# Feed-forward gate and up: both products with the weights' rounded half as one product of 512 columns, its two halves added on ScalarE and VectorE

## The reference

```python
def _swiglu(h, w_gate, w_up, w_down):      # h [256, 1024], inner width 2816
    return (silu(h @ w_gate) * (h @ w_up)) @ w_down

for l in range(2):
    mod = silu(c) @ w_mod[l] + b_mod[l]     # 9 rows of 1024: shift, scale, gate, three times
    x = x + 0.5 * g1 * _swiglu(_rmsnorm_2(x) * (1 + sc1) + sh1, gate1, up1, down1)
    x = x + g2 * _hybrid_mixer(...)
    x = x + 0.5 * g3 * _swiglu(_rmsnorm_2(x) * (1 + sc3) + sh3, gate2, up2, down2)
```

## Time and profile before

| | us |
|---|---|
| median of 3 runs | 1724.25 (1721.18 to 1724.79) |
| the profiled execution: its own time | 1718.4 |
| its span, first to last instruction | 1716.4 |
| TensorE, VectorE, ScalarE, GpSimd busy in the span | 1568.0, 979.8, 602.5, 205.0 |
| granted TensorE clock, mean over the span | 0.953 |

### The profile page before, as it was taken

One profiled execution on the slowest core, in us unless ns is written; L12 is line 12 of the kernel. 1 busy time (PEld: TensorE's weight loads), 2 busy tenths in 40 slices (PEclk: granted clock), 3 DMA queues, 4 the chain that ended last, 5 costly groups with the idle time before them and its releaser, 6 DMA issues.

```text
span 1716.4 us, 21728 instructions
## 1 busy us (share of the span) xinstructions
PE 1568.0 (91%) x8944; PEld 1232.6 (72%) x8944; DVE 979.8 (57%) x1482; ACT 602.5 (35%) x944; POOL 205.0 (12%) x205
## 2 busy tenths in 40 slices
PE   7997779898779998999989998989989999989998
PEld 1646356546459996786459997789977865479986
DVE  0376776767247776355427777677774453354444
ACT  2335121142134442253224443344433541144442
POOL 0021142000001110033001110001100241001100
PEclk9998979996799999999999999999999999989999
DMA  9444324166247877332337787668874323355551
GB/s 344 145 128 142 98 74 148 62 220 216 78 150 254 285 269 279 104 132 74 123 98 245 258 310 272 240 197 270 284 297 168 109 88 99 109 161 184 185 172 49
DMA packets 192106, 305.44 MB, mean 178 GB/s; under 512 B 6140, under 2 KB 116488, under 8 KB 191880
## 3 DMA queue, kind: packets, MB, share of 16 engines
q1 hardware_dynamic: 189088, 299.45, 51.5%
q10 hardware_dynamic: 2919, 4.61, 0.7%
HBM read 302.99 MB, written 1.05 MB: 177 GB/s over the span
## 4 chain that ended last, share of the span: by engine, by line
PE 76%; DVE 11%; ACT 7%; issue 2%; DMA 2%; POOL 1%; ACTq 0%; DVEq 0%; POOLq 0%
PE ps L373 75%; DVE accs L514 2%; PE ps L376 1%; DVE wlo L1948 1%; ACT whi L1906 1%; DMA ring<-in_ffn_w_down_dram 1%; DMA ring<-in_w_mod_dram 1%; DVE arena L1205 1%; DVE arena L1202 1%; DVE H L1729 1%; ACT arena L1440 0%; DVE H L1795 0%; POOL misc L1776 0%; DVE misc L1507 0%; ACT hhi L1911 0%
## 5 line engine op out<-in xcount | busy, mean ns | idle before, releaser
L1948 DVE TENSOR_TENSOR wlo<-ring,whi 128x1024 fp32r<-128x1024 f32 x264 | 322.6, 1225 | 235.4 <-ACT whi L1906 230.4
L373 PE MATMUL ps<-hhi,whi 128*128 128x256 f32 x1408 | 405.4, 288 | 21.2 <-DVE hlo L1954 16.0
L373 PE MATMUL ps<-hlo,whi 128*128 128x256 f32 x1408 | 401.8, 285 | 0.0
L373 PE MATMUL ps<-hhi,wlo 128*128 128x256 f32 x1408 | 401.6, 285 | 0.0
L1906 ACT ACTIVATE whi<-ring 128x1024 fp32r<-128x1024 f32 x264 | 275.2, 1055 | 310.0 <-PE ps L373 280.2
L373 PEld LDWEIGHTS ps<-hhi,whi 128*128 128x128 f32 x1408 | 273.9, 195 | 23.1 <-DVE hlo L1954 21.9
L373 PEld LDWEIGHTS ps<-hlo,whi 128*128 128x128 f32 x1408 | 274.0, 195 | 1.2 <-issue 1.2
L373 PEld LDWEIGHTS ps<-hhi,wlo 128*128 128x128 f32 x1408 | 273.7, 194 | 0.0
L373 PE MATMUL ps<-ring,H 128*128 128x512 f32 (+1 forms) x608 | 262.9, 583 | 11.0 <-ACT arena L2083 5.6
L373 PEld LDWEIGHTS ps<-ring,H 128*128 128x128 f32 x608 | 113.1, 193 | 129.4 <-issue 114.1
L514 DVE SCALAR_TENSOR_TENSOR accs<-ring,misc,accs 128x512 f32<-128x512 f32 x266 | 201.3, 757 | 3.0
(11 more groups left out here) (288 smaller groups left out, 1398.9 us busy)
## 6 DMA issues: line engine op xcount, KB each, us to landing
ring<-in_w_mod_dram SPq DMA_DIRECT2D x84, 1024.0 KB, 7.3
ring<-in_w_in_dram SPq DMA_DIRECT2D x48, 1024.0 KB, 5.0
ring<-in_ffn_w_gate_dram SPq DMA_DIRECT2D x44, 1024.0 KB, 6.8
ring<-in_ffn_w_up_dram SPq DMA_DIRECT2D x44, 1024.0 KB, 5.4
ring<-in_ffn_w_down_dram SPq DMA_DIRECT2D x44, 1024.0 KB, 6.6
ring<-in_w_out_dram SPq DMA_DIRECT2D x12, 1024.0 KB, 4.9
gates<-in_b_mod_dram SPq DMA_DIRECT2D x7, 512.0 KB, 6.6
ring<-in_w_proj_a_dram SPq DMA_DIRECT2D x2, 1024.0 KB, 5.9
```

The source lines that it names most:

```text
L373: return self.e.matmul(o, lhsT, rhs, start=start, stop=stop)
L1948: v.done(v.e.tensor_tensor(lo, M.slot(key)[:, r0:r0 + rn, :], plain(hi), ALU.subtract), ("split", l, sub, n), *([M.freed(key)] if ends els ...
```

## The change

- The two products that use whi become one: hhi and hlo now lie in one tensor (`HH`, 2 x 8 x 256), and one product of 512 columns takes both. `wlo*hhi` stays a product of 256 columns. So per weight block there are two products in place of three.
- A tile now needs two banks, one for gate and one for up. In each, columns 0 to 255 hold `whi*hhi + wlo*hhi` and columns 256 to 511 `whi*hlo`. The pool "ga" has six banks, handed out by two: a pair takes four. They are asked for one tile at a time, at q = 0.
- The two halves have to be added: ScalarE copies columns 256 to 511 of both banks to a scratch tile of 2 x 256 (128 x 512 elements), VectorE adds columns 0 to 255 of both banks to it and frees the banks. Silu is then taken from the scratch tile, in place, and the mult reads both halves of the scratch tile.
- Order: on both engines the work on a pair's results now comes before the piece q = 3 of the next pair instead of behind it, and goes by kinds: ScalarE copy, copy, silu, silu, ahi, ahi; VectorE add, add, mult, mult. The first tile is announced by TensorE before the second has ended.

```diff
 POOLS:
-"ga": (0, 1, 2, 3),
+"ga": range(6),
 Store:
-        self.HHI, self.HLO = self.sbr("hhi", [128, 8, 256]), self.sbr("hlo", [128, 8, 256])
+        self.HH = self.sbr("hh", [128, 2, 8, 256])
+        self.HHI, self.HLO = self.HH[:, 0, :, :], self.HH[:, 1, :, :]
 def spare(M):
-    return [M.H[:, k, 256:512] for k in range(8)]
+    return [M.H[:, 2 * i:2 * i + 2, 256:512] for i in range(3)]
...
     ps_ = pieces(l, sub)
     for f in range(0, 22, 2):
         for q in range(4):
+            if q == 3:
+                yield f
             if f < 20:
                 emit(ps_[4 * (f // 2) + 4 + q])
             elif q < 3:
                 emit(ps_[44 + q])
             if work is not None:
                 tick(work, beside(f, q))
-        yield f
     emit(ps_[47])
     for kt in range(19):
         yield ("down", kt)
...
 def act_ffn(a, l, sub):
     M = a.M
-    SG = spare(M)[0:3]
+    SG = spare(M)
     def emit(p):
         n, key, r0, rn, wd_, _ = p
...
     for p in first[1:]:
         emit(p)
     for f in split_all(a, l, sub, emit, None):
-        for j in range(2 if isinstance(f, int) else 0):
-            i, key = (f + j) % 3, ("gu", l, sub, f + j)
-            a.wait_ge(("gu", l, sub, f), ("alo", l, sub, f + j - 3))
-            a.done(a.e.activation(SG[i], M.ps(key)[:, 0:256], ACT.Silu), ("silu", l, sub, f + j))
+        pair = range(f, f + 2) if isinstance(f, int) else ()
+        for x in pair:
+            key = ("gu", l, sub, x)
+            b = M.banks[key, 0]
+            a.wait_ge(key, ("alo", l, sub, x - 3))
+            a.done(a.e.activation(SG[x % 3], M.psum[:, b:b + 2, 256:512], ACT.Copy), ("copied", l, sub, x))
+        for x in pair:
+            a.wait_ge(("summed", l, sub, x))
+            a.done(a.e.activation(SG[x % 3][:, 0, :], SG[x % 3][:, 0, :], ACT.Silu), ("silu", l, sub, x))
+        for j, x in enumerate(pair):
+            i = x % 3
             a.wait_ge(("act", l, sub, f + j))
-            a.done(a.e.activation(M.AHI[:, f + j, :], SG[i], ACT.Copy), ("ahi", l, sub, f + j))
+            a.done(a.e.activation(M.AHI[:, f + j, :], SG[i][:, 0, :], ACT.Copy), ("ahi", l, sub, f + j))
 def pool_ffn(g, l, sub):
     M = g.M
-    SG = spare(M)[0:3]
+    SG = spare(M)
     for f in range(22):
         g.wait_ge(("ahi", l, sub, f))
-        g.op(g.e.tensor_tensor(M.ALO[:, f, :], SG[f % 3], plain(M.AHI[:, f, :]), ALU.subtract), ("alo", l, sub, f))
+        g.op(g.e.tensor_tensor(M.ALO[:, f, :], SG[f % 3][:, 0, :], plain(M.AHI[:, f, :]), ALU.subtract), ("alo", l, sub, f))
 def v_ffn(v, l, sub, work):
     M = v.M
-    SG = spare(M)[0:3]
+    SG = spare(M)
     def emit(p):
         n, key, r0, rn, wd_, ends = p
...
     for f in split_all(v, l, sub, emit, work):
         for j in range(2 if isinstance(f, int) else 0):
             i, key = (f + j) % 3, ("gu", l, sub, f + j)
+            b = M.banks[key, 0]
+            v.wait_ge(("copied", l, sub, f + j))
+            v.done(v.e.tensor_tensor(SG[i], SG[i], M.psum[:, b:b + 2, 0:256], ALU.add), ("summed", l, sub, f + j),
+                   ("free", (key, 0)), ("free", (key, 1)))
+        for j in range(2 if isinstance(f, int) else 0):
+            i = (f + j) % 3
             v.wait_ge(("silu", l, sub, f + j))
-            v.done(v.e.tensor_tensor(SG[i], SG[i], M.ps(key)[:, 256:512], ALU.mult), ("act", l, sub, f + j), ("free", key))
+            v.done(v.e.tensor_tensor(SG[i][:, 0, :], SG[i][:, 0, :], SG[i][:, 1, :], ALU.mult), ("act", l, sub, f + j))
 def pe_ffn(pe, l, sub, work):
     M = pe.M
     for f in range(0, 22, 2):
-        bs = [pe.bank(("gu", l, sub, f + j), "ga") for j in range(2)]
         for q in range(4):
             n = 2 * f + q
             hi, lo = piece(M, n, 256)
-            o0, k0 = 256 * (q // 2), 4 * (q % 2)
+            k0 = 4 * (q % 2)
             pe.wait_ge(("split", l, sub, n), ("hlo", l, sub, q % 2))
             for j in range(2):
-                c = slice(j * 128, j * 128 + 128)
-                for kt in range(4):
-                    ins = pe.mm3(bs[j][:, o0:o0 + 256], (hi[:, kt, c], lo[:, kt, c]), (M.HHI[:, k0 + kt, :], M.HLO[:, k0 + kt, :]),
-                                 k0 + kt == 0, k0 + kt == 7)
-            pe.done(ins, ("staged", l, sub, n), *([("gu", l, sub, f)] if q == 3 else []))
+                c, key = slice(j * 128, j * 128 + 128), ("gu", l, sub, f + j)
+                if q == 0:
+                    for i in range(2):
+                        pe.bank((key, i), "ga")
+                b = M.ps((key, q // 2))
+                for kt in range(k0, k0 + 4):
+                    low = lambda: pe.mm(b[:, 0:256], lo[:, kt - k0, c], M.HHI[:, kt, :], False, False)
+                    if kt:
+                        low()
+                    ins = pe.mm(b, hi[:, kt - k0, c], M.HH[:, :, kt, :], kt == 0, kt == 7)
+                    if kt == 0:
+                        low()
+                if q == 3 and j == 0:
+                    pe.done(ins, key)
+            pe.done(ins, ("staged", l, sub, n), *([key] if q == 3 else []))
             tick(work, beside(f, q))
     bs = [[pe.bank(("d", l, sub, blk, hf), "down") for hf in range(2)] for blk in range(2)]
     for k0 in range(19):
```

More of the change, by code:

```diff
@@ L155 @@
 NS = 5
-POOLS = {"all": range(8), "six": range(6), "mods": (6, 7), "rest": (0, 1), "att": (2, 3, 4, 5), "bo": (7,), "row": (6,), "sq": (4, 5, 6, 7), "low": (0, 1), "skk": (2,), "mod3": (3,), "sdec": (4, 5), "sq2": (6, 7), "ga": (0, 1, 2, 3),
+POOLS = {"all": range(8), "six": range(6), "mods": (6, 7), "rest": (0, 1), "att": (2, 3, 4, 5), "bo": (7,), "row": (6,), "sq": (4, 5, 6, 7), "low": (0, 1), "skk": (2,), "mod3": (3,), "sdec": (4, 5), "sq2": (6, 7), "ga": range(6),
          "down": (2, 3, 4, 5), "chain": (2, 3, 4, 5), "proj": (0, 1), "rec": (2, 3), "sd": (4, 5, 6), "dbo": (7,), "outx": (2, 3, 0, 1), "ds": (4, 5, 6, 7), "turnf": (6, 7, 0, 1), "turnx": (6, 7, 4, 5)}
```

## The result

The kernel after took 1716.73 us (median of 9 executions, 1713.59 to 1720.4) against 1723.59 us for the kernel before on the same chip (9 executions, 1718.66 to 1726.75): ratio 0.9969 [0.9956, 0.9982], so 3 to 8 us faster, where 15.1 us were forecast. 1716 is what rivals B and C gave.

The account below looks back on a forecast made before the run. TensorE's own pace of products was taken to bound the kernel. Gains of 6.6 us in the first three feed-forwards and 8.5 in the last sum to 15.1, from 1724.25 to 1709.2 us; range with rivals 1700 to 1722.

Parts of the forecast that it names:

- rival B: Gate and up: the 512-column product with two runs costs 240 ns, TensorE gains nothing, only stage ends gain: 1716 us; 7%.
- Rival C: Steps and banks eat all the gain in the first three feed-forwards, the last keeps 8.5 us: 1716 us; 17%.
- the end of gate and up: Before down in the first three: next transfer at 126.1 to 126.7 us, TensorE waits of 1.3, 2.4 and 1.9 us.
- TensorE's pace: Gate and up: a block falls from 360.0 to 346.7 ns, 13.3 ns less, 4.69 us for 352, 18.8 for all four.
- The last feed-forward: No modulation steps: gains 4.7 us on TensorE, 2.0 of idle before down and 1.8 of clock, 8.5 us together.
- VectorE's turn: Pairs with steps: first add to next wlo 3.65 us for 3.02; a turn 11.33 us with 4 steps, 12.11 with 5.
- rival A: VectorE becomes the bound in the three feed-forwards with steps, from an average turn of 11.95 us: 1735 us; 9%.
- The table load: First silu of each of the first three feed-forwards stands behind the copies, its table load no longer hidden: 0.5 us each.
- The sum: Whole kernel: 6.6 us gained in the first three feed-forwards and 8.5 in the last, 15.1 us: 1709.2 us.
- Rival D: Gate and up: later release of up slots starves ScalarE by 1 us a pair, 30 us slower, about 1745 us; 3%.

Follow-up runs that it names:

- experiment 1: Kernel after with the two halves of h interleaved, so the 512 moving columns are one run: 1717.74 us, 0.9977 to the kernel before.
- experiment 3: Kernel after without copies and adds, silu and mult reading columns 0 to 255 from PSUM: 1699.97 us, 0.9863 to the kernel before.
- experiment 4: Kernel after with down's first two transfers issued earlier, at q = 0 and 2 of the last pair: 1707.97 us, 0.9917 to the kernel before.
- experiment 8: Kernel after with down's first two transfers early and down's banks from the rotation of six, per token block: 1695.67 us, 0.9838 to the kernel before.
- experiment 7: Kernel before, narrow products, with only the work on a pair's results moved ahead of q = 3: 1712.73 us, 0.9937 to the kernel before.
- experiment 9: Kernel before, narrow products, with work on a pair's results ahead of q = 3 and down's first two transfers early: 1712.21 us, 0.9941.

## Why the prediction was too high

The change is two things, and my sum mixed them. The new order is worth 11 us on narrow products, and the wide products without it cost 7%; inside it, at the surroundings of the change, they cost 5.5 us. Two steps of the prediction failed: the 13.3 ns a block on TensorE, which are 8.0, and above all the working of the end of gate and up, where a gain for the first three was to come from and where there were longer waits. Point by point:

**TensorE's pace: wrong by size.** "13.3 ns, 4.69 us for 352" was a sum of distances, each measured beside products of its own width. As one product of each width the block takes 352 ns, a gain of 8.0 ns, 2.8 us a feed-forward. The floor of about 2.5 ns beyond the columns that the Trainium skill states (TensorE: Matmul & The Clock Gate, "Wait — 56ns, not 53.3ns?") would give 2.5 ns a block; the traces show 8.0, between the page's and mine. Rival B's reason, the two runs, fell with experiment 1.

**The last feed-forward: right in kind, 6.1 us of 8.5.** Its pairs give 129.2 - 126.4 = 2.8 us for 4.7, the gap before down 1.8 for 2.0, and the clock, from 61.3 to 59.8 us of down with no product at half clock, 1.5 for 1.8.

**VectorE's turn: the step that failed in the middle of the stage.** The 3.65 us from the first add to the next wlo are there (3.63 us from the add at 560.54), but only on a turn that VectorE enters late. On the turn after a short one it is back at TensorE's heels, the second add waits 0.47 us for its copy, and the same stretch is 551.73 - 547.55 = 4.18 us. So the turn with 5 steps took 12.99 us: by my terms 12.11 - 0.26 + 0.61 = 12.46, and these 0.5 us more. The average turn is 12.1 us, just above the 11.95 from which, by rival A, VectorE decides; over the nine middle pairs of all three it is 12.04. The nine middle pairs of the first three feed-forwards went from 108.0, 108.1 and 108.0 us to 109.3, 107.3 and 108.4, +0.3 on average where I had about 1 us less. Rival A was thus partly right: with the copies and adds out (experiment 3) the nine pairs take 105.7 us, so VectorE's work and the banks that wait for it set the pace of the stage, though at TensorE's old speed and not at 12.4.

**The end of gate and up: the largest miss.** I gave "126.1, 126.3 and 126.7 us" for the next transfer against 128.2 and 132.0 before, with waits of 1.3, 2.4 and 1.9 us in front of down. The waits were 3.3, 3.1 and 3.1 and the transfer came at 132.5, 130.2 and 132.3 (in the first 146.6, less the first pair of 14.1). The working had VectorE's instructions back to back there and checked only a gate transfer for its 14.5 us of lead. Down's first weights had none: ScalarE waited 3.16 us for them, and the adds of the last pair, and with them down's banks, stand behind those pieces. I had the first of these adds 118.8 us after the first pair's end. It comes at 123.3, and with the transfers early (experiment 4) at 120.9: the weights made it 2.4 us late, the longer turns before them the other 2.1. Experiments 4 and 8 separate weights and banks: the early transfers gain 9 us, and the banks, until then worth nothing, another 14 by the ratios (0.9917 to 0.9838).

**The table load.** The 0.5 us that I put for it in each of the three stood without a row. The trace has a table load of 1.28 us before the first silu of the first feed-forward alone, and one turn later a pair is 0.8 us longer than in the other two.

**The sum.** In the profiled stages the first three came out at +5.0 for -6.6 us, the last at -6.1 for -8.5. Rival C has it in kind: steps and banks ate the gain of the first three, though no gate transfer came late. That 1716.7 is also its number, and that of rival B, is in part chance: by B TensorE gains nothing, and by C the last feed-forward keeps 8.5 us and not 6.1. What I missed entirely is that taking the adds' cost of 18 us (experiment 3) and the order's gain of 11 apart would have shown a forecast made of two large terms of opposite sign. Rival D, transfers, was priced at 1 us a pair and given 3%. In the pairs it didn't come about: after the first pair ScalarE's only waits for transfers are on down's. There, at one place in each of three feed-forwards, they decided.

## What to carry to other kernels

When a change alters the arithmetic and moves work in an order, price the move by itself: here it was worth more than the whole. Check the lead of the first transfers of the next stage, not of one in the middle, before costing a wait in front of that stage. And a fix that measures as nothing (the banks) may only stand behind another wait: try it again once that is gone.

## What the runs showed of the hardware

The pace of a product is not fixed by its width. Narrow gate and up give 120.0 ns for 256 columns and down gives 226.7 ns for 512; in the wide gate and up it is 116.7 and 235.3 ns when the widths alternate, and 118.9 and 232.2 in groups of four. The neighbour alone does not decide it: where two 512-column products of the kernel after follow one another, they start 235.8 ns apart (141 cases), and a second 256 columns starts 116.0 ns after the first (160 cases). The sum of 351 to 352 ns holds in three arrangements, with the moving operand in one run or two; why it is not 346.7 stays open.

At half clock a 512-column product of down takes 427 ns for 227. In the last down 7 of the first products ran so after TensorE had idled 2.15 us (before, and narrow with early transfers), none after 0.25 us or less. Idle time before down does not decide it alone: the second down ran its first 50 us at full clock after 2.22 us idle (experiments 7 and 9), and in experiment 3 all three did throughout after 1.4 to 2.2 us. After 2.9 us or more 12 of 13 downs lost some of their first 20 us to half clock.
